# Silu in one ScalarE instruction for the gates and HGRN's queries, in a two-block, three-mixer fp32 kernel

## The reference, cut to what matters

```python
def hgrn2_mixer(q, f_fwd, f_bwd, i, lb, norm_g):
    qh = heads(jax.nn.silu(q), HA)
...
        y_a = hgrn2_mixer(a_q, a_ff, a_fb, a_i, lbs[l], hgrn_norm_g[l]) * jax.nn.silu(a_g)
        y_b = retention_mixer(b_q, b_k, b_v, ret_norm_g[l], ret_norm_b[l]) * jax.nn.silu(b_g)
        y_c = rwkv7_mixer(c_s, rwkv_mu[l], rwkv_w0[l], rwkv_w_lora_b[l], rwkv_a0[l],
                          rwkv_a_lora_b[l], rwkv_k_k[l], rwkv_k_a[l], rwkv_r_k[l],
                          rwkv_ln_g[l], rwkv_ln_b[l]) * jax.nn.silu(c_g)
```

## Time and profile before

| | |
|---|---|
| median of 3 runs | 3730.78 us (3728.26 to 3735.71) |
| the profiled execution, its own time | 3736.72 us |
| its span | 3734.7 us |
| PE busy | 3535.5 us (95%) |
| DVE busy | 1335.7 us (36%) |
| ACT busy | 720.5 us (19%) |
| GpSimd busy | 43.5 us (1%) |
| mean granted clock of TensorE | 0.97 |
| the mixers of layer 0, about | 65 to 1190 us of the span |
| the mixers of layer 1, about | 1260 to 2378 us |

### The profile page before, as it was taken

How to read it: one execution, slowest core, us unless ns; L and a number is a source line. 1 busy time by engine, 2 the same in 40 slices (tenths; PEclk the granted TensorE clock), 3 DMA queues, 4 the chain that set the end, 5 groups by cost and what they waited for, 6 DMA issues and landing times.

```text
span 3734.7 us, 43111 instructions
## 1 busy us (share of the span) xinstructions
PE 3535.5 (95%) x18508; PEld 2956.0 (79%) x18508; DVE 1335.7 (36%) x2779; ACT 720.5 (19%) x1360; POOL 43.5 (1%) x51
## 2 busy tenths in 40 slices
PE   7997999998999999999999999899989988997999
PEld 6997988998987898898898898686658747855684
DVE  3546546537410463655645531100130012015100
ACT  2223222313100232322313210100010011002100
POOL 0000000000000000000000000000000000000000
PEclk9998999999999999998999999999989989997999
DMA  4112122112124321211212122444434423431343
GB/s 183 57 68 71 68 71 79 57 71 91 68 105 150 121 68 68 94 68 49 80 68 84 67 91 102 142 152 153 147 102 139 154 99 124 147 126 68 113 151 108
DMA packets 53117, 375.55 MB, mean 101 GB/s; under 512 B 6049, under 2 KB 6177, under 8 KB 9025
## 3 DMA queue, kind: packets, MB, share of 16 engines
q1 hardware_dynamic: 51376, 368.01, 28.4%
q0 software_dynamic: 1552, 4.79, 0.4%
HBM read 371.72 MB, written 1.05 MB: 100 GB/s over the span
## 4 chain that ended last, share of the span: by engine, by line
PE 90%; DVE 7%; ACT 1%; issue 1%; DMA 1%; SPq 0%; ACTq 0%; DVEq 0%
PE bank L418 42%; PE bank L1635 11%; PE bank L1572 6%; PE bank L435 5%; PE bank L721 5%; PE bank L743 4%; PE bank L732 4%; PE bank L1194 1%; DVE rw_score L998 1%; PE bank L456 1%; PE bank L660 1%; PE bank L1458 1%; PE bank L772 1%; PE bank L708 1%; PE bank L756 1%
## 5 line engine op out<-in xcount | busy, mean ns | idle before, releaser
L418 PE MATMUL bank<-h_features,weight_ring 128*128 128x256 f32 x7072 | 1594.4, 383 | 16.6 <-DMA weight_ring<-in_w_in 9.7
L418 PEld LDWEIGHTS bank<-h_features,weight_ring 128*128 128x128 f32 x7072 | 1335.0, 191 | 200.8 <-issue 13.5
L1635 PE MATMUL bank<-weight_ring,ff_act 128*128 128x512 f32 x704 | 303.1, 592 | 4.7 <-DVE ff_act L1718 4.7
L1635 PEld LDWEIGHTS bank<-weight_ring,ff_act 128*128 128x128 f32 x704 | 133.4, 190 | 172.7 <-issue 166.5
L1718 DVE TENSOR_TENSOR ff_act<-ff_silu,bank 128x256 f32<-128x256 f32 x88 | 37.1, 421 | 577.2 <-ACT ff_silu L1709 577.2
L721 PE MATMUL bank<-rw_bm,rw_score 128*128 128x64 f32 x1536 | 206.5, 278 | 7.2 <-DVE rw_bm L1023 3.7
L721 PEld LDWEIGHTS bank<-rw_bm,rw_score 128*128 128x128 f32 x1536 | 194.7, 196 | 13.7 <-issue 3.4
L435 PE MATMUL bank<-weight_ring,h_features 128*128 128x256 f32 (+2 forms) x896 | 202.5, 375 | 2.0 <-DVE h_features L501 2.0
L743 PE MATMUL bank<-rw_ex,rw_sig 128*128 128x64 f32 x1536 | 203.6, 276 | 0.0
L1023 DVE COPY_PREDICATED rw_bm<-mask_constants,bank 128x256 f32<-128x256 uint32 x160 | 78.6, 491 | 330.8 <-PE bank L732 330.4
L743 PEld LDWEIGHTS bank<-rw_ex,rw_sig 128*128 128x128 f32 x1536 | 191.6, 194 | 1.4
(11 more groups left out here) (420 smaller groups left out, 3592.3 us busy)
## 6 DMA issues: line engine op xcount, KB each, us to landing
weight_ring<-in_w_in SPq DMA_DIRECT2D x146, 1024.0 KB, 4.9
weight_ring<-in_f00w SPq DMA_DIRECT2D x33, 1024.0 KB, 4.9
weight_ring<-in_f01w SPq DMA_DIRECT2D x33, 1024.0 KB, 4.8
weight_ring<-in_f10w SPq DMA_DIRECT2D x33, 1024.0 KB, 4.9
weight_ring<-in_f11w SPq DMA_DIRECT2D x33, 1024.0 KB, 4.9
weight_ring<-in_w_b SPq DMA_DIRECT2D x16, 1024.0 KB, 5.0
weight_ring<-in_w_out SPq DMA_DIRECT2D x16, 1024.0 KB, 5.2
weight_ring<-in_conv_in SPq DMA_DIRECT2D x10, 1024.0 KB, 4.8
```

Source lines behind the costliest of these rows:

```text
L418: m = e.matmul(bank[:, j, :], w[:, k, j * P:(j + 1) * P], x[:, k, :], start=k == 0, stop=k == kt - 1, skip_group_check=True)
L1635: m = e.matmul(banks[i], src[:, k0 + k, t * P:(t + 1) * P], w[:, k, s * 512:(s + 1) * 512], start=k0 + k == 0, stop=k0 + k == k_tiles - 1, ...
```

## The change

ACT computes Silu straight from the bank at the four places and frees the bank itself. The four kinds of DVE product are gone. The tables of `ORDER` for both mixer stages are replaced on PE, DVE, ACT and SP (first line of some of them shown). Nothing else differs; the PE generators are the same.

```diff
 ORDER = {
     ("mixers0", "tensor"):
-        "H2 R20 H2 R5 H12 R9 H R3 H R4 H R4 H3 R4 B R3 B H R B R3 B R2 H2 R2 B R2 B R4 H2 R8 B R3 B2 R3 H2 R3 B R "
...
+        "H2 R21 H R4 H8 R6 H R5 H R H R4 H R4 H R4 H R4 H R5 H R2 H3 R2 B R4 B R6 H R2 B R3 B R3 B R4 H2 R3 B R "
...
     ("mixers0", "sync"):
-        "H R4 H4 B6 H5 R4 B3 H B H2 B H B H R4 B6 H4 B3 H B2 R4 B6 H2 B H B H B H R4 B R H B R H B R H B R ",
+        "H R4 H4 B6 H5 R4 B3 H2 B H B H B H R4 B6 H2 B H B H R4 B H B7 H B H B R2 H B R H B R H B R H B R H B R H "
...
-        e.activation(R.gate, pairs(g.banks.get(f"c_g{q}", l)), ACT.Sigmoid).then_inc(*act.up(f"c_g{q}", l))
+        e.activation(R.gate, pairs(g.banks.get(f"c_g{q}", l)), ACT.Silu).then_inc(*act.up(f"c_g{q}", l))
+        g.banks.empty(act, f"c_g{q}", l)
...
-        e.wait_ge(*act.at(f"c_g{q}", l))
-        e.tensor_tensor(R.gate, R.gate, pairs(g.banks.get(f"c_g{q}", l)), ALU.mult).then_inc(*dve.up(f"c_g{q}", l))
-        g.banks.empty(dve, f"c_g{q}", l)
-        yield
...
-        e.activation(H.q, pairs(g.banks.get(f"a_q{q}", l)), ACT.Sigmoid).then_inc(*act.up(f"a_q{q}", l))
+        e.activation(H.q, pairs(g.banks.get(f"a_q{q}", l)), ACT.Silu).then_inc(*act.up(f"a_q{q}", l))
+        g.banks.empty(act, f"a_q{q}", l)
...
-        e.activation(H.gate, pairs(g.banks.get(f"a_g{q}", l)), ACT.Sigmoid).then_inc(*act.up(f"a_g{q}", l))
+        e.activation(H.gate, pairs(g.banks.get(f"a_g{q}", l)), ACT.Silu).then_inc(*act.up(f"a_g{q}", l))
+        g.banks.empty(act, f"a_g{q}", l)
...
-            e.activation(B.gate[:, 2 * s:2 * s + 2, :], pairs(g.banks.get(f"b_g{q}{s}", l)), ACT.Sigmoid).then_inc(
+            e.activation(B.gate[:, 2 * s:2 * s + 2, :], pairs(g.banks.get(f"b_g{q}{s}", l)), ACT.Silu).then_inc(
                 *act.up(f"b_g{q}{s}", l))
+            g.banks.empty(act, f"b_g{q}{s}", l)
```

More of the change, by code:

```diff
@@ L225 @@
     ("mixers0", "sync"):
-        "H R4 H4 B6 H5 R4 B3 H B H2 B H B H R4 B6 H4 B3 H B2 R4 B6 H2 B H B H B H R4 B R H B R H B R H B R ",
+        "H R4 H4 B6 H5 R4 B3 H2 B H B H B H R4 B6 H2 B H B H R4 B H B7 H B H B R2 H B R H B R H B R H B R H B R H "
+        "B R ",
     ("mixers1", "sync"):
-        "R4 H5 B6 H5 R4 B6 H5 B3 R4 B4 H3 B H B H B3 R4 B5 H2 B H B H B H B H B R6 H B R H B R ",
+        "R4 H5 B6 H5 R4 B6 H5 B3 R4 B3 H2 B H B H B H B3 R4 B5 H2 B H B H B H R4 B R H B R H B R H B R ",
     ("conv", "sync"):
@@ L1282, in hgrn_dve @@
         yield
-        e.wait_ge(*act.at(f"a_q{q}", l))
-        e.tensor_tensor(H.q, H.q, pairs(g.banks.get(f"a_q{q}", l)), ALU.mult).then_inc(*dve.up(f"a_q{q}", l))
-        g.banks.empty(dve, f"a_q{q}", l)
-        yield
         for d, (name, key, b) in enumerate((("a_ff", H.kf, H.bf), ("a_fb", H.kb, H.bb))):
@@ L1300, in hgrn_dve @@
             yield
-        e.wait_ge(*act.at(f"a_g{q}", l))
-        e.tensor_tensor(H.gate, H.gate, pairs(g.banks.get(f"a_g{q}", l)), ALU.mult).then_inc(*dve.up(f"a_g{q}", l))
-        g.banks.empty(dve, f"a_g{q}", l)
-        yield
         for n in range(2):
@@ L1523, in retention_dve @@
             e.tensor_tensor(z, z, rot, ALU.add).then_inc(*dve.up("rot", l, q, s))
-        for s in range(2):
-            yield
-            e.wait_ge(*act.at(f"b_g{q}{s}", l))
-            gate = B.gate[:, 2 * s:2 * s + 2, :]
-            e.tensor_tensor(gate, gate, pairs(g.banks.get(f"b_g{q}{s}", l)), ALU.mult).then_inc(*dve.up())
-            g.banks.empty(dve, f"b_g{q}{s}", l)
-            yield
         for h in range(2):
```

## The result

| | before | with the change |
|---|---|---|
| median of 4 runs | 3729.55 us | 3753.67 us |
| lowest to highest | 3728.26 to 3735.71 | 3749.95 to 3756.16 |
| the profiled execution | 3736.72 us | 3753.14 us |
| ratio, 95% interval | 1 | 1.0061 [1.0043, 1.0078] |
| TensorE's mean clock | 0.97 | 0.965 |

The kernel became slower by 24 us between the medians, where 17 were predicted (3748 us, 3714 to 3775).

A forecast was written before the change was run, and what follows sets the result against it. PE, busy 95% of the span, was taken as the bound. Stalls +18.5, clock and functions 0, remainder -2 gave about +17 us on the median 3730.8, so 3748 us, range 3714 to 3775 us.

The forecast's parts named there:

- my signs: Listed observations that would show the forecast right, such as 171 loads, DVE less by 27 us, setup stalls of 12-16 us.
- the loads off the path: ACT's 17 extra table loads, 22 us, were taken to delay PE nowhere; the opposing slower rival, 3770 us, had chance 0.15.
- The stalls: PE's idle time in RWKV's setups in both mixers, claimed to grow from 26.3 to 44.8 us, by 18.5 us.
- the remainder: 60 us of matmuls leaving the setups run elsewhere at no cost; filling waits there was to save 2 us.
- the count: Each setup's PE idle time from L647 to L677, taken as the chain's length less the cover; 44.8 us in all.
- the cover: Other streams' matmuls that PE's order puts between L647 and L677; 197 us before, 137 us after, over all setups.
- The clock: TensorE's low-clock time in the mixers: more behind long stalls, less behind short waits, claimed to cancel to no change.
- each long stall: Long PE waits in RWKV's setups, three instead of one, at 7 us of clock each: +14 us.
- the four short waits: PE's waits in front of L647, claimed to go, returning 2 to 5 us of clock each, 14 us in the middle.
- The functions: 40 sigmoids on ACT become 40 Silus at the same cost, claimed to change nothing.
- of the other products I count nothing: DVE's removed products other than the gate's L917 were claimed to win nothing, since PE waits for nothing they write.
- The faster rival: PE's scattered mixer waits and their clock loss go, saving 35 us to 3713 us; chance 0.2.

The follow-up runs named there:

- silu_old_tables: Silu without the DVE products, as in the changed kernel, but in the ORDER tables of the kernel before; 3721.3 us, 0.9975 of the kernel before.
- early_square: The changed kernel with k squared behind c_k's shift, its sum inside v's projection, the square root ahead of the gate; 3750.3 us, 1.0051 of before.

## Why the prediction was right, and where not

**The direction and the cause.** Right. The loss is the new tables of `ORDER` (32 us of it, silu_old_tables), and it lies in the mixers. Right too: no wait before L647, 171 loads, ACT +21.4 us (about 22 predicted), the loads off the path, no wait for ACT in front of L732 or L743 over 0.5 us. Three of my signs were missed: DVE's work fell by 19.8 us, not 27, PE's idle time in the mixers grew by 8.6 us, not 15 to 20, and layer 0's q = 1 waits 9.7 us, not 12 to 16. The total, 3748 against 3753.7 us, is closer than its terms were, and that is luck.

**The stalls, predicted +18.5 us, then 2 off for the remainder.** Measured: idle time +8.6 us in the mixers. Setup by setup the count held within 2 us: q = 2 of layer 0 15.4 us (15.7), q = 1 9.7 us (11.5), layer 1 q = 3 12.4 us (14.4) and q = 2 3.0 us (2.6); q = 0 of layer 0 has none (0.6). Layer 0's q = 1 shows what the count missed. PE's timeline there:

```profile
334.76 2.05 PE L1177 MATMUL bank<-hg_q,hg_ks 128*128 128x128 f32 x8 [5.14 <-DVE hg_ks L1315]
341.36 3.75 PE L1449 MATMUL bank<-rt_vt,rt_gam 128*128 128x256 f32 x8 [4.55 <-issue]
344.91 1.92 PE L1191 MATMUL bank<-hg_qs,hg_ks 128*128 128x128 f32 x8
```

The chain from L647 took 346.75 - 320.44 = 26.3 us, not 23.8. But at 1.2 GHz the cover lasts twice as long (L1449 3.75 us against 1.89), so part of the chain passed under slow matmuls instead of idle time: it moved from the stall to the clock. Its wait "issue" of 4.55 us ends 0.1 us after DVE's L1520 (340.58 to 341.26), which writes the rt_gam that L1449 reads: it is B's step in DVE's order that PE waits for there.

The setups' stalls are 40.4 us, so they grew by 40.4 - 26.3 = 14.1 us, not 18.5. The other mis-sized term is the *remainder*: PE's waiting outside these stalls fell from 81.2 - 26.3 = 54.9 us to 89.8 - 40.4 = 49.4 us, 5.5 us where I took off 2. Waits that I had not named came (3.5 us before L1557; two waits for weights grew from 2.2 to 4.9 and from 2.4 to 4.1 us), and more of the old ones went, the issue wait of 5.1 us before L1458 in layer 1 among them.

By layer the forecast was wrong. Its stalls were 0.6 + 11.5 + 15.7 - 22.5 = +5.3 us in layer 0 and 2.6 + 14.4 - 3.8 = +13.2 us in layer 1. Idle time did grow by 5.2 us in layer 0, but by only 3.4 us in layer 1, where other waits went; and the 12.1 us that the clock took on top fell on layer 0, where my terms for it cancel.

**The clock, predicted 0.** Measured +10.1 us between these profiles; this is the term that failed. I gave each long stall 7 us of clock and took back 14 us for the four short waits. PE's work at 1.2 GHz directly around the three long stalls, halved, is 5.9 us for layer 0's q = 1, 2.8 us for q = 2 and 7.9 us for layer 1's q = 3, together about 16.5 us, against 7.1 us around before's one: +9.4 where I had +14. All other stretches made 38.7 us before and 39.3 us now, where I had 14 us less. This split rests on a choice: the stretch at 361.26, 10 us of loss, begins 14.5 us after the first scores of layer 0's q = 1, and counted with that stall it would make the long stalls +19 and the others -9. The sum of the two, +10.1 against 0, does not depend on it. The stretches behind the old waits before L647 are gone, such as the one at 579, but new ones came in the ladders, as at 361 and 934. That four short waits go doesn't give their clock back if the new order puts other short waits elsewhere. Since before's profile is 7 us over its median, the clock's usual share of the loss may be larger; no run here shows it.

**The functions, predicted 0.** Measured -9.7 us in the old tables. The step "of the other products I count nothing" was wrong, in the direction that I had named as possible, unless the gain comes from the banks that are free earlier, which I had put at nothing as well. DVE fell by 24.1 us with Silu in the old tables (1335.7 to 1311.6 us), which is 40 times the 0.6 us net of overlap that I used for such an operation elsewhere, and not 40 times 0.68; the new order gives back 4.3 of them, which I can't explain. So the sum came near by two errors against each other: functions 0 instead of -10, tables +17 instead of +32.

**The faster rival** named the right mechanism (scattered waits and their clock go), and it is what silu_old_tables shows. It failed for the change because the mixers' mean clock fell to 0.96 and 0.97; the rival needed 0.99.

## What to carry to other kernels

When a change brings new instructions and a new order together, run the new instructions in the old order first: here the edit won 0.25%, the order that came with it lost 0.86%, and one could have been kept without the other. With fixed orders on several engines, an earlier result helps only if the place that waits for it moves too (early_square). Count the cover of a wait from PE's order, but add the clock: short waits in busy code can cost more through the clock than by their length (2.2 us of waits ahead of the stretch at 361, 10 us lost in it).

## What the runs showed of the hardware

Around the 14.3 us stall the clock was low for only 5.6 us of PE's work (589.96 to 607.02). The costliest stretches follow short waits: at 361.26 the clock fell after waits of 0.6, 0.9, 0.2 and 0.5 us since 351 (it had been low for 3.4 us from 354.4 on already), and stayed at 0.50 for 20.5 us with PE busy for 20.0 of them. The one at 1719.77, with 17.6 us of work, came after waits of 0.6 and 0.7 us, and a wait of 2.2 us fell into it. I had expected a higher price for the long waits: 7 us for each, against 2 to 5 us for one of 2 us.

Nothing follows a load here: the one at 584.66 takes 1.28 us, and the sigmoid starts at 585.95. The Trainium skill, "ScalarE: Activation LUTs", section "What ACT_TABLE_LOAD costs", adds a drain of about 1.38 us; this trace does not show it, as the one of before did not. Silu and Sigmoid don't share a table (171 loads against 155 in the same order), yet 16 loads, 20.5 us of ACT, gave no difference that can be told in the new order, nor did 12 in the old one. In the setup of q = 2 above, DVE's reciprocal of 512 float32 elements takes 3.35 us, as long as five other operations of its size.
